# Up projection with the weights stationary and 256 token columns moving

## Chip, cores and metric

One core of a Trainium2 chip runs the whole kernel in one launch. The metric is the device time in microseconds; lower is better.

## Reference, cut to what matters

x is (1, 256, 2048), all in float32: 256 tokens, 2048 channels. After the token mixers, which the change does not touch, the channel mixer is

```python
h = rmsnorm(x, g_ffn_pre[l])
u = causal_dwconv(h @ w_up[l], ffn_conv_w[l])      # w_up: 2048 x 11264, 3 taps over the tokens
gate, val = jnp.split(u, 2, axis=-1)               # 5632 channels each
x = x + rmsnorm((jax.nn.silu(gate) * val) @ w_down[l], g_ffn_post[l])
```

rmsnorm divides each token's row by its root mean square. The kernel multiplies the un-normalised rows, and applies the token's factor r_h2 to the product.

## The kernel before

Every projection is made from three products of float32r parts: w is split into w_hi (rounded to float32r) and w_lo (the rest), and so are the activations; the product is hi*hi + hi*lo + lo*hi. Weights stream from memory in blocks of 256 x 512 (512 KB) through rings of four buffers: SyncE loads `raw`, ScalarE writes `w_hi` (line 415), VectorE writes `w_lo` (line 670), TensorE multiplies. A buffer of `raw` is free again when `w_lo` is written, one of `w_hi` and `w_lo` when the multiplication of four blocks earlier is done (`block_done`).

`multiply` (line 987) takes one block: for each of its 2 groups of 128 input channels and each of the 2 tiles of 128 tokens, three matmuls with a 128x128 tile of the transposed activations as stationary operand and 512 weight columns as moving operand: 12 matmuls a block, each with its own weight load. The result is 128 tokens x 512 channels in a PSUM bank, tokens on partitions.

The up projection runs in 11 steps (`up_step`), each with a half of 512 gate channels and a half of 512 value channels, 8 blocks a half, so 176 blocks. The convolution runs over tokens and wants channels on partitions. So each half takes this way: ScalarE copies the two banks to `up_stage`, scaled by r_h2 (`up_evacuate`, line 584, 2 instructions); TensorE turns it with 8 transposes of 128x128 into `TURN` in PSUM (`up_turn`, line 1159, placed behind the second block of the next half); ScalarE makes the first tap from it (`up_first_tap`, line 591, 4 instructions); VectorE adds the other two taps (`turned_conv`, line 703, 8 instructions). After both halves come silu (line 636), the product (906) and its split into act_hi (606) and act_lo (909), which the down projection reads. Gate and value halves have their own PSUM banks (`ACC[0]`, `ACC[1]`).

The order of work on each engine is written by hand: these steps stand at fixed places i = 0..7 between the block splits of the following half. The last `up_turn` stands inside the first chunk of the down projection. Before step 0, x is renewed, turned (line 1185) and split into h2_hi, h2_lo (the buffers of hT_hi, hT_lo, whose names the trace shows), and GpSimd works out r_h2 (line 366).

Of the kernel before, what the change touches and what calls it, by code (L numbers as in the profile page):

```python
# [7 lines left out]
ALU = mybir.AluOpType  # L8
# [3 lines left out]
P = 128  # L12
NT = 2
# [3 lines left out]
KB = 2  # L17
# [6 lines left out]
def build_block_kernel(nc, x, mem, g_mix_pre, w_in, w_gate, b_gate, conv_w, w_conv_out,  # L24
# [47 lines left out]
    with ExitStack() as ctx:  # L72
        def sem(name):
            return ctx.enter_context(nc.semaphore(name))
# [11 lines left out]
        def at(name, offset, shape, dt=F32):  # L86
            return nc.alloc_sbuf_tensor_at(name, shape, dt, offset=base + offset)
# [105 lines left out]

        act_hi = at("act_hi", RB, [P, FK, TOK], F32R)
        act_lo = at("act_lo", RB + 44 * K, [P, FK, TOK], F32R)
        up_stage = at("up_stage", RB + 88 * K, [P, NT, CW])
# [37 lines left out]
        d_inv, d_scaled, d_a, d_aT, d_aT_sb, d_o = (sem(n) for n in ("d_inv", "d_scaled", "d_a", "d_aT", "d_aT_sb", "d_o"))  # L234
        d_sq, d_ms, d_r, d_on, d_oT, d_hi, d_lo = (sem(n) for n in ("d_sq", "d_ms", "d_r", "d_on", "d_oT", "d_hi", "d_lo"))
        gate_ready, gated_sum, mix_hi = (sem(n) for n in ("gate_ready", "gated_sum", "mix_hi"))
        mix_sq, mix_sum, x_new, h2_sq = (sem(n) for n in ("mix_sq", "mix_sum", "x_new", "h2_sq"))
        silu_done, prod_done, act_hi_done, act_lo_done = (sem(n) for n in ("silu_done", "prod_done", "act_hi_done", "act_lo_done"))
        down_sq, down_y, down_sum, out_ready, out_stored = (sem(n) for n in ("down_sq", "down_y", "down_sum", "out_ready", "out_stored"))
# [163 lines left out]
        def _(act):  # L403
# [177 lines left out]
                    if i == 5 and c == 0:  # L581
                        merge_hi(NCH - 1)

            def up_evacuate(k, n_end, parity):
                act.wait_ge(turned_done, k)
                act.wait_ge(block_done, n_end)
                for t in range(NT):
                    last = nc.scalar.activation(up_stage[:, t, :], ACC[parity][:, t, :], ACT.Copy, scale=r_h2[:, t:t + 1])
                last.then_inc(evacuated[parity], 1)

            def up_first_tap(k, dst, blk):
                act.wait_ge(turned_done, k + 1)
                for b in range(BPC):
                    last = nc.scalar.activation(dst[:, b, :], TURN[:, b, :], ACT.Copy, scale=up_taps[:, 2, bass.ds(blk + b, 1)])
                last.then_inc(tap0, 1)

            def value_done(j, i):

                if i == 3:
                    up_evacuate(T_UP + 2 * j + 1, N_UP + 2 * CB * j + 2 * CB, 1)  # L600
                if i == 5:
                    act.wait_ge(prod_done, AHEAD + j)
                    up_first_tap(T_UP + 2 * j + 1, conv_v, FK + BPC * j)
                if i == 7:
                    act.wait_ge(prod_done, AHEAD + j + 1)
                    nc.scalar.activation(act_hi[:, bass.ds(BPC * j, BPC), :], prod[:], ACT.Copy).then_inc(act_hi_done, 1)

            def up_step(j, jp):
                n = N_UP + 2 * CB * j
                for i in range(CB):  # L610
                    split(n, i)
                    if jp is not None:
                        value_done(jp, i)
                    elif i == 2:

                        mix_squares(NCH - 1)
                        for g in range(NCH):
                            prepare(2 * NCH + g, g, (SCORE_T, TURN)[g % 2], g_ffn_v, h2_hi)
                        for t in range(NT):
                            act.wait_ge(mix_sq, NT * NCH + t)  # L620
                            last = nc.scalar.activation(junk_wide[:], x_res[:, t, :], ACT.Square, accum_out=sq_h2[:, t:t + 1])
                            last.then_inc(mix_sq, 1)
                        act.wait_ge(mix_sq, NT * NCH + NT)
                for i in range(CB):
                    split(n, CB + i)
                    if i == 3:
                        if jp is None:
                            act.wait_ge(rms_ready, 4)
                        up_evacuate(T_UP + 2 * j, n + CB, 0)
                    if i == 5:  # L630
                        if jp is not None:
                            act.wait_ge(prod_done, AHEAD + j)
                        up_first_tap(T_UP + 2 * j, conv_g, BPC * j)
                    if i == 6:
                        act.wait_ge(turned_read, T_UP + 2 * j + 1)
# [30 lines left out]
        def _(dve):  # L666
            def split(n, i, inc=1):

                dve.wait_ge(hi_ready, n + i + 1)
                nc.vector.tensor_tensor(w_lo[i % RING][:], raw[i % RING][:], w_hi[i % RING][:].bitcast(F32),  # L670
                                        ALU.subtract).then_inc(lo_ready, inc)
# [43 lines left out]

            def conv_count(k):

                if isinstance(k, int) and k < T_UP:
                    return [TI[("cv", 0)], TI[("cv", 1)]].index(k)
                return k - T_UP + 2  # L720

            def after_projection(c, i):
                name, half = proj[c]
# [164 lines left out]
            for c in range(NCH):  # L888
                for i in range(CB):
# [6 lines left out]
                    if i == 5 and c == 0:  # L896
                        merge_lo(NCH - 1)

            def value_done(j, i):
                if i == 5:  # L900
                    turned_conv(T_UP + 2 * j + 1, conv_v, lambda m, b: up_taps[:, m, bass.ds(FK + BPC * j + b, 1)])
                if i == 6:
                    dve.wait_ge(turned_read, T_UP + 2 * j + 2)
# [30 lines left out]
            def up_step(j, jp):  # L934
                n = N_UP + 2 * CB * j
                for i in range(CB):
                    split(n, i)
                    if jp is not None:
                        value_done(jp, i)
                    elif i == 2:  # L940
                        new_x()
                for i in range(CB):
                    split(n, CB + i)
                    if i == 5:
                        turned_conv(T_UP + 2 * j, conv_g, lambda m, b: up_taps[:, m, bass.ds(BPC * j + b, 1)])

            up_step(0, None)
            with dve.Fori(1, NUP) as j:
# [37 lines left out]
        def _(pe):  # L986
# [169 lines left out]
                    if i == 1 and c == 0:  # L1156
                        turn_merged(T_MERGE + NCH - 1)

            def up_turn(k, parity, count):
                pe.wait_ge(evacuated[parity], count)  # L1160
                pe.wait_ge(turned_read, k)
                turn(up_stage, TURN, turned_done)

            def up_step(j, jp):
                n = N_UP + 2 * CB * j
                pe.wait_ge(evacuated[0], E_UP + j)
                for i in range(CB):
                    if jp is None:
                        pe.wait_ge(prep_lo, 4 * NCH + i + 1)
                    multiply(n, i, CB, h2_hi, h2_lo, lambda t: ACC[0][:, t, :])  # L1170
                    if i == 1 and jp is not None:
                        up_turn(T_UP + 2 * jp + 1, 1, E_UP + jp + 1)
                pe.wait_ge(evacuated[1], E_UP + j)
                for i in range(CB):
                    multiply(n + CB, i, CB, h2_hi, h2_lo, lambda t: ACC[1][:, t, :])
                    if i == 1:
                        up_turn(T_UP + 2 * j, 0, E_UP + j + 1)

            for g in range(NCH):
                if g % 2:  # L1180
# [18 lines left out]
            pe.wait_ge(evacuated[0], E_DN)  # L1199
            down_chunk(0, lambda t: PS[:, t, :])  # L1200
            pe.wait_ge(turned_read, T_UP + 2 * NUP)
# [26 lines left out]
```

## Time and profile before

| | us |
|---|---|
| median of 3 runs (1712.16 to 1712.39) | 1712.18 |
| profiled execution, span from first to last instruction | 1710.7 |
| TensorE matmuls, busy | 1681.2 (98%) |
| TensorE weight loads, busy | 1389.9 (81%) |
| VectorE, busy | 956.0 (56%) |
| ScalarE, busy | 808.0 (47%) |
| DMA engines, share of the span | 59.2% |

The span is 1.5 us shorter than the median of the runs: that much lies around it. A matmul's duration in the trace is longer than the distance to the start of the next, because matmuls are pipelined; what a stream of them costs is read from the starts. TensorE's work therefore has to be counted by starts, not by busy time. Weight loads have a row of their own, PEld, beside the matmuls. A float32 matmul (not float32r) is recorded as two passes; a transpose as one.

### The profile page before, as it was taken

The numbers are of one execution on the slowest core, as the hardware profiler recorded it, in microseconds if no ns is written. First come the engines' busy times: TensorE is split into PE (matmuls) and PEld (weight loads), VectorE is DVE, ScalarE is ACT, GpSimd is POOL, SyncE is SP. The second block draws the span as 40 slices with busy tenths as digits, with TensorE's granted clock in tenths as the row PEclk, the third lists the DMA queues.
The fourth block names the chain that finished last, engine by engine and source line by source line (L and its number), as shares of the span: only waits on it lengthen the run. The fifth ranks groups of instructions, "written<-read, shape, count | busy, mean of one in ns | idle before, by whom it ended". The sixth has DMA issues, their size and how long they took to land.

```text
span 1710.7 us, 21909 instructions
## 1 busy us (share of the span) xinstructions
PE 1681.2 (98%) x7645; PEld 1389.9 (81%) x7645; DVE 956.0 (56%) x1100; ACT 808.0 (47%) x1028; POOL 21.4 (1%) x49
## 2 busy tenths in 40 slices
PE   8999999999999999999999899999999999999997
PEld 6888888888888888888888688888888888888886
DVE  5554555544556656655555566665666666544544
ACT  5544444444444444444444455555555555443442
POOL 0000000000000000000000000000000000000000
PEclk9999999999999999999999899999999999999999
DMA  7656555666655655666555366666666665654653
GB/s 270 205 176 186 168 159 163 186 192 185 190 187 189 239 179 178 196 219 198 186 199 189 123 180 187 182 189 189 186 185 185 184 183 185 214 194 171 211 196 123
DMA packets 165518, 320.87 MB, mean 188 GB/s; under 512 B 10504, under 2 KB 10841, under 8 KB 164953
## 3 DMA queue, kind: packets, MB, share of 16 engines
q1 hardware_dynamic: 165433, 320.15, 59.2%
q8 instruction: 34, 0.56, 0.1%
q14 instruction: 19, 0.16, 0.0%
q10 hardware_dynamic: 32, 0.01, 0.0%
HBM read 318.02 MB, written 2.10 MB: 187 GB/s over the span
## 4 chain that ended last, share of the span: by engine, by line
PE 95%; DVE 3%; ACT 1%; issue 1%; DMA 0%; DVEq 0%; ACTq 0%
PE PS L997 28%; PE PS L999 28%; PE PS L998 28%; PE PS L1140 3%; PE PS L1139 3%; PE PS L1138 3%; PE PS L1006 3%; ACT w_hi L415 0%; PE PS L1080 0%; PE PS L1065 0%; DVE y_down L979 0%; DMA mem_sb<-in_mem_dram 0%; ACT p_diff L540 0%; DVE x_res L925 0%; DVE gated L798 0%
## 5 line engine op out<-in xcount | busy, mean ns | idle before, releaser
L670 DVE TENSOR_TENSOR w_lo<-raw,w_hi 128x1024 fp32r<-128x1024 f32 x584 | 712.8, 1225 | 681.1 <-ACT w_hi L415 680.0
L415 ACT ACTIVATE w_hi<-raw 128x1024 fp32r<-128x1024 f32 x584 | 616.4, 1059 | 770.0 <-PE PS L999 717.2
L997 PE MATMUL PS<-w_hi,hT_hi 128*128 128x512 f32 x1536 | 606.1, 395 | 0.0
L999 PE MATMUL PS<-w_hi,hT_lo 128*128 128x512 f32 x1536 | 599.0, 390 | 0.0
L998 PE MATMUL PS<-w_lo,hT_hi 128*128 128x512 f32 x1536 | 598.3, 389 | 0.0
L999 PEld LDWEIGHTS PS<-w_hi,hT_lo 128*128 128x128 f32 x1536 | 288.6, 188 | 61.0
L997 PEld LDWEIGHTS PS<-w_hi,hT_hi 128*128 128x128 f32 x1536 | 288.9, 188 | 60.5 <-issue 2.7
L998 PEld LDWEIGHTS PS<-w_lo,hT_hi 128*128 128x128 f32 x1536 | 289.0, 188 | 58.1
L997 PE MATMUL PS<-w_hi,act_hi 128*128 128x512 f32 x352 | 137.2, 390 | 0.0
L999 PE MATMUL PS<-w_hi,act_lo 128*128 128x512 f32 x352 | 137.0, 389 | 0.0
L998 PE MATMUL PS<-w_lo,act_hi 128*128 128x512 f32 x352 | 136.9, 389 | 0.0
L997 PEld LDWEIGHTS PS<-w_hi,act_hi 128*128 128x128 f32 x352 | 66.1, 188 | 14.2 <-issue 0.6
L999 PEld LDWEIGHTS PS<-w_hi,act_lo 128*128 128x128 f32 x352 | 66.1, 188 | 13.7
L998 PEld LDWEIGHTS PS<-w_lo,act_hi 128*128 128x128 f32 x352 | 66.1, 188 | 13.6
L997 PE MATMUL PS<-w_hi,memT_hi 128*128 128x512 f32 x128 | 51.6, 403 | 1.5 <-DVE w_lo L670 0.9
L999 PE MATMUL PS<-w_hi,memT_lo 128*128 128x512 f32 x128 | 50.8, 397 | 0.0
L998 PE MATMUL PS<-w_lo,memT_hi 128*128 128x512 f32 x128 | 50.8, 397 | 0.0
L997 PE MATMUL PS<-w_hi,mixT_hi 128*128 128x512 f32 x128 | 49.9, 390 | 0.0
L999 PE MATMUL PS<-w_hi,mixT_lo 128*128 128x512 f32 x128 | 49.8, 389 | 0.0
L998 PE MATMUL PS<-w_lo,mixT_hi 128*128 128x512 f32 x128 | 49.8, 389 | 0.0
L997 PEld LDWEIGHTS PS<-w_hi,memT_hi 128*128 128x128 f32 x128 | 24.6, 192 | 7.0 <-issue 1.3
L999 PEld LDWEIGHTS PS<-w_hi,memT_lo 128*128 128x128 f32 x128 | 24.6, 192 | 5.3
(172 smaller groups left out, 1111.5 us busy)
## 6 DMA issues: line engine op xcount, KB each, us to landing
raw<-in_w_up_dram SPq DMA_DIRECT2D x176, 512.0 KB, 4.4
raw<-in_w_in_dram SPq DMA_DIRECT2D x112, 512.0 KB, 3.7
raw<-in_w_gate_dram SPq DMA_DIRECT2D x96, 512.0 KB, 4.1
raw<-in_w_down_dram SPq DMA_DIRECT2D x88, 512.0 KB, 4.2
raw<-in_w_mem_kv_dram SPq DMA_DIRECT2D x32, 512.0 KB, 4.1
raw<-in_w_o_dram SPq DMA_DIRECT2D x32, 512.0 KB, 3.6
raw<-in_w_conv_out_dram SPq DMA_DIRECT2D x16, 512.0 KB, 3.5
raw<-in_w_cross_out_dram SPq DMA_DIRECT2D x16, 512.0 KB, 3.7
```

The lines of the kernel that those rows point to most:

```text
L415: nc.scalar.activation(w_hi[i % RING][:], raw[i % RING][:], ACT.Copy).then_inc(hi_ready, inc)
L670: nc.vector.tensor_tensor(w_lo[i % RING][:], raw[i % RING][:], w_hi[i % RING][:].bitcast(F32), ALU.subtract).then_inc(lo_ready, inc)
L997: nc.tensor.matmul(o, a_hi, b_hi, start=first, stop=False)
L998: nc.tensor.matmul(o, a_hi, b_lo, start=False, stop=False)
L999: last = nc.tensor.matmul(o, a_lo, b_hi, start=False, stop=last_k)
L1006: last = nc.tensor.transpose(dst[:, b, t * P:(t + 1) * P], src[:, t, b * P:(b + 1) * P], ident[:])
L1138: nc.tensor.matmul(ACC[1][:, t, :], hi[:, k, s], w_hi[i % RING][:, c, :], start=k == 0, stop=False)
L1139: nc.tensor.matmul(ACC[1][:, t, :], hi[:, k, s], w_lo[i % RING][:, c, :], start=False, stop=False)
L1140: last = nc.tensor.matmul(ACC[1][:, t, :], lo[:, k, s], w_hi[i % RING][:, c, :], start=False, stop=k == HK - 1)
```

## The change

In the up projection alone, operands change places: a 128x128 tile of w_hi or w_lo is the stationary operand, and the 256 tokens of h2 move. The output has 128 channels on partitions and 256 tokens in half a PSUM bank. `multiply_up` issues for each block 2 groups of input channels x 4 groups of output channels x 3 products = 24 matmuls of 256 columns, each with its weight load, where `multiply` issued 12 of 512. Transposes, `up_stage` and its two ScalarE copies a half go. r_h2 now varies along the free axis, so it has to be a row that is the same on all partitions: once, VectorE writes two diagonal matrices, TensorE multiplies them with ones (float32, 2 matmuls of 128 columns), and ScalarE copies the row out of PSUM (`r_row`). VectorE then scales each half with one instruction over 128x1024 (`up_scale`, at i == 2), PSUM to SBUF. The taps read this SBUF copy and not PSUM; the first tap moves from i == 5 to i == 4. The down projection is as before, but for the transposes that stood in its first chunk.

```diff
+        up_scaled_sb = at("up_scaled_sb", RB + 88 * K, [P, BPC, TOK])
...
+        UP = [PS[:, 2 * h:2 * h + 2, :].rearrange("p b (c t) -> p (b c) t", t=TOK) for h in range(2)]
...
-            def up_evacuate(k, n_end, parity):
-                act.wait_ge(turned_done, k)
-                act.wait_ge(block_done, n_end)
-                for t in range(NT):
-                    last = nc.scalar.activation(up_stage[:, t, :], ACC[parity][:, t, :], ACT.Copy, scale=r_h2[:, t:t + 1])
-                last.then_inc(evacuated[parity], 1)
...
             def up_first_tap(k, dst, blk):
-                act.wait_ge(turned_done, k + 1)
+                act.wait_ge(up_scaled, k + 1)
                 for b in range(BPC):
-                    last = nc.scalar.activation(dst[:, b, :], TURN[:, b, :], ACT.Copy, scale=up_taps[:, 2, bass.ds(blk + b, 1)])
+                    last = nc.scalar.activation(dst[:, b, :], up_scaled_sb[:, b, :], ACT.Copy, scale=up_taps[:, 2, bass.ds(blk + b, 1)])
                 last.then_inc(tap0, 1)
...
+                    if i == 0 and jp is None:
+                        act.wait_ge(r_row_turned, 1)
+                        nc.scalar.activation(r_row[:], PS[:, 4, 0:TOK], ACT.Copy).then_inc(r_row_done, 1)
...
+            def up_scale(k, n_end, half):
+
+                dve.wait_ge(block_done, n_end)
+                if isinstance(k, int) and k == 0:
+                    dve.wait_ge(r_row_done, 1)
+                nc.vector.tensor_tensor(up_scaled_sb[:], UP[half], r_row[:, None, :].to_broadcast([P, BPC, TOK]),
+                                        ALU.mult).then_inc(up_scaled, 1)
+
+            def up_conv_taps(k, dst, taps):
+
+                dve.wait_ge(tap0, k + 3)
+                for b in range(BPC):
+                    last = nc.vector.scalar_tensor_tensor(out=dst[:, b, 1:TOK], in0=up_scaled_sb[:, b, 0:TOK - 1], scalar=taps(1, b),
+                                                          in1=dst[:, b, 1:TOK], op0=ALU.mult, op1=ALU.add)
...
+                    elif i == 4:
+
+                        dve.wait_ge(rms_ready, 4)
+                        nc.vector.memset(ones[:], 1.0)
+                        for t in range(NT):
+                            last = nc.vector.tensor_scalar(r_diag[:, t, :], ident[:], r_h2[:, t:t + 1], None, ALU.mult)
+                        last.then_inc(r_diag_done, 1)
...
-            def up_turn(k, parity, count):
-                pe.wait_ge(evacuated[parity], count)
-                pe.wait_ge(turned_read, k)
-                turn(up_stage, TURN, turned_done)
+            def multiply_up(n, i, half):
+
+                pe.wait_ge(lo_ready, n + i + 1)
+                for c in range(KB):
+                    k = KB * i + c
+                    for b in range(BPC):
+                        s = slice(b * P, (b + 1) * P)
+                        o, last_k = UP[half][:, b, :], k == DK - 1
+                        b_hi, b_lo = w_hi[i % RING][:, c, s], w_lo[i % RING][:, c, s]
+                        nc.tensor.matmul(o, b_hi, h2_hi[:, k, :], start=k == 0 and b % 2 == 0, stop=False, skip_group_check=True)
+                        nc.tensor.matmul(o, b_hi, h2_lo[:, k, :], start=False, stop=False, skip_group_check=True)
+                        last = nc.tensor.matmul(o, b_lo, h2_hi[:, k, :], start=False, stop=last_k, skip_group_check=True)
+                last.then_inc(block_done, 1)
...
+                    multiply_up(n, i, 0)
+                    if jp is None and i == CB - 1:
+
+                        pe.wait_ge(r_diag_done, 1)
+                        for t in range(NT):
+                            last = nc.tensor.matmul(PS[:, 4, t * P:(t + 1) * P], ones[:], r_diag[:, t, :], start=True, stop=True)
+                        last.then_inc(r_row_turned, 1)
...
-                    if i == 1 and isinstance(j, int):
-                        up_turn(T_UP + 2 * NUP - 1, 1, E_UP + NUP)
```

## Rows read from the trace of the kernel before

**Rows 1.** Page, part 1: busy us (share of the span) x instructions.

```profile
PE 1681.2 (98%) x7645; PEld 1389.9 (81%) x7645; DVE 956.0 (56%) x1100; ACT 808.0 (47%) x1028; POOL 21.4 (1%) x49
```

**Rows 2.** Page, part 2: TensorE clock granted, tenths, 40 slices.

```profile
PEclk9999999999999999999999899999999999999999
```

**Rows 3.** Page, part 4: chain that ended last, shares by engine.

```profile
PE 95%; DVE 3%; ACT 1%; issue 1%; DMA 0%; DVEq 0%; ACTq 0%
```

**Rows 4.** Groups by line and shape: count | busy us, mean ns | idle before.

```profile
L997 PE MATMUL PS<-w_hi,hT_hi 128*128 128x512 f32 x1536 | 606.1, 395 | 0.0
...
L1006 PE MATMUL PS<-ident,up_stage 128*128 128x128 f32 x176 | 22.8, 272 | 0.0
```

**Rows 5.** Timeline, TensorE, in an up step: start us, us, instruction.

```profile
1000.20 0.39 PE L997 MATMUL PS<-w_hi,hT_hi 128*128 128x512 f32 x1
...
1003.83 0.39 PE L998 MATMUL PS<-w_lo,hT_hi 128*128 128x512 f32 x1
```

**Rows 6.** Timeline, weight loads beside those matmuls.

```profile
1000.21 0.19 PEld L998 LDWEIGHTS PS<-w_lo,hT_hi 128*128 128x128 f32 x1
1000.43 0.19 PEld L999 LDWEIGHTS PS<-w_hi,hT_lo 128*128 128x128 f32 x1
```

**Rows 7.** Stretches: us, busy by engine, PEclk, DMA share, GB/s; an up stretch.

```profile
1000.00:1100.00 100.00, 100.00 (x459) 83.12 (x458) 60.12 (x72) 53.47 (x66) 0.00 (x0) 1.00 0.63 188
```

**Rows 8.** Timeline, TensorE, around one group of transposes.

```profile
1010.86 0.39 PE L999 MATMUL PS<-w_hi,hT_lo 128*128 128x512 f32 x1
1011.09 1.03 PE L1006 MATMUL PS<-ident,up_stage 128*128 128x128 f32 x8
1011.88 0.48 PE L997 MATMUL PS<-w_hi,hT_hi 128*128 128x512 f32 x1
1012.19 0.40 PE L998 MATMUL PS<-w_lo,hT_hi 128*128 128x512 f32 x1
```

**Rows 9.** Timeline, TensorE, first matmuls of up step 0.

```profile
960.32 0.63 PE L998 MATMUL PS<-w_lo,hT_hi 128*128 128x512 f32 x1
...
962.03 0.63 PE L999 MATMUL PS<-w_hi,hT_lo 128*128 128x512 f32 x1
```

**Rows 10.** Stretch of those matmuls: the eighth figure is the clock.

```profile
960.30:962.40 2.10, 2.10 (x6) 1.65 (x5) 1.40 (x4) 2.10 (x5) 0.00 (x0) 0.50 0.00 0
```

**Rows 11.** Timeline, weight loads with 128-column float32 matmuls, then float32r ones.

```profile
455.99 0.30 PEld L1123 LDWEIGHTS PS<-v_tok,a_diffT 128*128 128x128 f32 x2
456.21 0.30 PEld L1124 LDWEIGHTS PS<-v_tok,a_diffT 128*128 128x128 f32 x2
456.43 0.19 PEld L997 LDWEIGHTS PS<-w_hi,hT_hi 128*128 128x128 f32 x1
456.55 0.19 PEld L998 LDWEIGHTS PS<-w_lo,hT_hi 128*128 128x128 f32 x1
```

**Rows 12.** Timeline, TensorE, the same place: float32 passes of 128 columns.

```profile
455.88 0.38 PE L1122 MATMUL PS<-v_tok,a_diffT 128*128 128x128 f32 x2
...
456.32 0.39 PE L1124 MATMUL PS<-v_tok,a_diffT 128*128 128x128 f32 x2
```

**Rows 13.** Groups by line and shape, 985 to 1460 us: VectorE and ScalarE.

```profile
L670 DVE TENSOR_TENSOR w_lo<-raw,w_hi 128x1024 fp32r<-128x1024 f32 x168 | 205.7, 1224 | 166.7 <-ACT w_hi L415 166.7
L415 ACT ACTIVATE w_hi<-raw 128x1024 fp32r<-128x1024 f32 x168 | 177.9, 1059 | 193.3 <-PE PS L999 193.3
...
L588 ACT ACTIVATE up_stage<-PS,r_h 128x512 f32<-128x512 f32 x41 | 25.7, 674 | 0.0
...
L707 DVE SCALAR_TENSOR_TENSOR conv_g<-PS,up_taps,conv_g 128x255 f32<-128x255 f32 x44 | 18.2, 476 | 4.2 <-ACT conv_g L594 4.2
...
L594 ACT ACTIVATE conv_g<-PS,up_taps 128x256 f32<-128x256 f32 x44 | 17.2, 475 | 0.0
```

**Rows 14.** One line of VectorE: a PSUM by SBUF product, 128x1024; min/median/max ns.

```profile
L746 DVE TENSOR_TENSOR y_tmp<-PS,convT x2: 1217/1217/1217, 291.0 to 313.6; 128x1024 f32<-128x1024 f32 x2
```

**Rows 15.** Timeline, GpSimd, then VectorE, start of up step 0.

```profile
966.27 0.69 POOL L366 TENSOR_TENSOR r_h<-mean_sq,minus_half 128x2 f32<-128x2 f32 x1
...
966.75 3.50 DVE L670 TENSOR_TENSOR w_lo<-raw,w_hi 128x1024 fp32r<-128x1024 f32 x3 [0.92 <-ACT w_hi L415]
```

More of the change, by code:

```diff
@@ L195, in build_block_kernel @@
         act_lo = at("act_lo", RB + 44 * K, [P, FK, TOK], F32R)
-        up_stage = at("up_stage", RB + 88 * K, [P, NT, CW])
+        up_scaled_sb = at("up_scaled_sb", RB + 88 * K, [P, BPC, TOK])
+        r_diag = at("r_diag", RB + 96 * K, [P, NT, P])
+        ones = at("ones", RB + 97 * K, [P, P])
+        r_row = at("r_row", RB + 104 * K + 2 * K, [P, TOK])
         conv_g = at("conv_g", RB + 92 * K, [P, BPC, TOK])
@@ L236, in build_block_kernel @@
         gate_ready, gated_sum, mix_hi = (sem(n) for n in ("gate_ready", "gated_sum", "mix_hi"))
+        r_diag_done, r_row_turned, r_row_done = (sem(n) for n in ("r_diag_done", "r_row_turned", "r_row_done"))
+        up_scaled, up_conv = sem("up_scaled"), sem("up_conv")
         mix_sq, mix_sum, x_new, h2_sq = (sem(n) for n in ("mix_sq", "mix_sum", "x_new", "h2_sq"))
@@ L716, in conv_count @@
             def conv_count(k):
-                if isinstance(k, int) and k < T_UP:
-                    return [TI[("cv", 0)], TI[("cv", 1)]].index(k)
-                return k - T_UP + 2
+                return [TI[("cv", 0)], TI[("cv", 1)]].index(k)
             def after_projection(c, i):
@@ L897, in _ @@
                         merge_lo(NCH - 1)
+            def up_scale(k, n_end, half):
[9 more added lines that the diff above has]
+                                                          in1=dst[:, b, 1:TOK], op0=ALU.mult, op1=ALU.add)
+                last.then_inc(tap1, 1)
+                dve.wait_ge(tap1, k + 3)
+                for b in range(BPC):
+                    last = nc.vector.scalar_tensor_tensor(out=dst[:, b, 2:TOK], in0=up_scaled_sb[:, b, 0:TOK - 2], scalar=taps(0, b),
+                                                          in1=dst[:, b, 2:TOK], op0=ALU.mult, op1=ALU.add)
+                last.then_inc(up_conv, 1)
             def value_done(j, i):
+                if i == 2:
+                    up_scale(2 * j + 1, N_UP + 2 * CB * j + 2 * CB, 1)
                 if i == 5:
-                    turned_conv(T_UP + 2 * j + 1, conv_v, lambda m, b: up_taps[:, m, bass.ds(FK + BPC * j + b, 1)])
+                    up_conv_taps(2 * j + 1, conv_v, lambda m, b: up_taps[:, m, bass.ds(FK + BPC * j + b, 1)])
                 if i == 6:
-                    dve.wait_ge(turned_read, T_UP + 2 * j + 2)
+                    dve.wait_ge(up_conv, 2 * j + 2)
                     dve.wait_ge(silu_done, j + 1)
@@ L941, in up_step @@
                         new_x()
+                    elif i == 4:
[4 more added lines that the diff above has]
+                        last.then_inc(r_diag_done, 1)
                 for i in range(CB):
                     split(n, CB + i)
+                    if i == 2:
+                        up_scale(2 * j, n + CB, 0)
                     if i == 5:
-                        turned_conv(T_UP + 2 * j, conv_g, lambda m, b: up_taps[:, m, bass.ds(BPC * j + b, 1)])
+                        up_conv_taps(2 * j, conv_g, lambda m, b: up_taps[:, m, bass.ds(BPC * j + b, 1)])
             up_step(0, None)
@@ L1157, in _ @@
                         turn_merged(T_MERGE + NCH - 1)
-            def up_turn(k, parity, count):
-                pe.wait_ge(evacuated[parity], count)
-                pe.wait_ge(turned_read, k)
-                turn(up_stage, TURN, turned_done)
+            def multiply_up(n, i, half):
+                pe.wait_ge(lo_ready, n + i + 1)
+                for c in range(KB):
+                    k = KB * i + c
+                    for b in range(BPC):
+                        s = slice(b * P, (b + 1) * P)
[5 more added lines that the diff above has]
+                last.then_inc(block_done, 1)
             def up_step(j, jp):
                 n = N_UP + 2 * CB * j
-                pe.wait_ge(evacuated[0], E_UP + j)
+                if jp is None:
+                    pe.wait_ge(evacuated[0], E_UP)
+                else:
+                    pe.wait_ge(up_scaled, 2 * jp + 1)
                 for i in range(CB):
@@ L1169, in up_step @@
                         pe.wait_ge(prep_lo, 4 * NCH + i + 1)
[L1170 to L1173, printed above, removed]
+                    multiply_up(n, i, 0)
[4 more added lines that the diff above has]
+                        last.then_inc(r_row_turned, 1)
+                if jp is None:
+                    pe.wait_ge(evacuated[1], E_UP)
+                else:
+                    pe.wait_ge(up_scaled, 2 * jp + 2)
                 for i in range(CB):
-                    multiply(n + CB, i, CB, h2_hi, h2_lo, lambda t: ACC[1][:, t, :])
-                    if i == 1:
-                        up_turn(T_UP + 2 * j, 0, E_UP + j + 1)
+                    multiply_up(n + CB, i, 1)
             for g in range(NCH):
```

20 lines of the change are left out of this document (7 added, 13 removed).

## Prediction

> **What bounds the kernel now.** I read the views in this order. Part 1 of the page shows TensorE busy 98% of the span and no other engine above 56% [rows 1]; the chain that ended last lies on TensorE for 95% [rows 3]; its clock is full nearly everywhere [rows 2]. So the kernel is a queue of matmuls, and an edit counts by what it does to that queue. In the groups by line the 512-column float32r matmuls have no idle time before them, and the transposes of the up stage have none either [rows 4]: those are paid in full. Then the timeline, for the price of one matmul. From 1000.20 to 1003.83 there are 16 steps from start to start, so one 512-column matmul costs 0.2267 us, not the 0.39 us of its record [rows 5]. Each has a weight load, which starts with the matmul before it and is recorded with 0.19 us [rows 6], so it is over before it is wanted. In an up stretch the clock is 1.00, DMA at 63% and VectorE at 60% [rows 7]: nothing else is close.
>
> **Removed: the transposes.** From the last matmul ahead of a group (1010.86) to the second one behind it (1012.19) are 1.33 us [rows 8]; two ordinary steps would be 0.45, so a group costs 0.88 us (8 transposes at about 0.11). There are 22 groups (176 transposes [rows 4]): 22 x 0.88 = 19.4 us less on the path. The ScalarE copies, 2 x 0.674 us a half [rows 13], are off the path and bring nothing.
>
> **Changed: the matmuls, which decide the case.** The up stage has 11 x 2 x 8 = 176 blocks. Before: 12 x 176 = 2112 matmuls x 0.2267 = 478.8 us. After: 24 x 176 = 4224 matmuls of 256 columns at a price P that the trace does not show, since all float32r matmuls in it have 512 columns. The columns streamed are the same, so the question is how the 0.2267 us splits into a part per column and a part per matmul.
> At half clock (0.50, the 1.2 GHz level [rows 10]) the steps are (962.03 - 960.32) / 4 = 0.4275 us [rows 9], which is 512 columns at one column a cycle with nothing above it. At 2.4 GHz one column a cycle would be 0.2134 us. The full-clock step has 0.0133 us above that. This excess is either
> a) per matmul (a start, or a clash with the one weight load that goes with each): P = 0.1067 + 0.0133 = 0.120 us, 4224 x 0.120 = 506.9 us, 28.1 us more;
> b) per column (a stream that can't quite be fed at full clock): P = 0.2267 / 2 = 0.1133 us, 478.8 us, no change.
> The bound below: a load must fit under a matmul. Loads with 128-column float32 passes follow each other at 0.11 us (455.99, 456.21, 456.43, two in each of the first two records), and the first float32r load is followed by the next after 0.12 [rows 11]; the passes themselves come every 0.11 us [rows 12]. So 0.111 us is the lowest P that I can defend: 4224 x 0.111 = 468.9 us, 9.9 less. The bound above: if stationary and moving reads share one path, 640 columns in 0.2267 us make 384 columns 0.136 us: 574.5 us, 95.7 more. The loads of rows 11 speak against this one, since they ran at their rate beside a stream.
> I take a). A hint for it: the step beneath which a transpose's load ran is 0.23 us (1010.86 to 1011.09 [rows 8]), and the steps behind a break are 0.23 too, so the excess moves with what surrounds a matmul, which a pure rate per column would not do. It is a weak hint, and b) keeps a good chance.
> The Trainium skill ("TensorE: Matmul & The Clock Gate", section "Wait — 56ns, not 53.3ns?") has a fixed cost of about 2.5 ns for each warm matmul, on top of columns / 2.4 GHz. As an estimate from that page P would be 0.109 us, the sum 461.4 us, and the kernel some 36 us faster with the transposes gone. The 512-column step of this trace, 0.2267 us, does not follow that figure (0.2158), so I don't forecast by it, and its result shares the chance of rival 2; what it says of the kind of the cost (per matmul) is my case a).
>
> **Added: the row of r_h2, once.** On TensorE 2 float32 matmuls of 128 columns, two passes each, 4 x 0.11 = 0.44 us [rows 12], with about 0.1 for the break: 0.5 us. The operands are early: r_h2 is ready at 966.96 and VectorE writes its third to fifth w_lo of this step from 966.75 [rows 15], so its three small instructions behind i == 4 come blocks ahead of the end of the half. ScalarE then waits at i == 0 of the second half, with the splits of that half's blocks 1 to 7 queued behind it, until the row is in PSUM. From the end of block 7: 0.65 us to the signal, a 128x256 copy 0.48, w_hi 1.06, w_lo 1.22 [rows 13], together 3.4 us. TensorE has the row's 0.5 us and block 0 of the second half, 24 x 0.120 = 2.9 us, that is 3.4 us before it needs this w_lo. I put 0.3 us for this race: 0.8 us in all. If it is lost outright, 1 us.
>
> **Added off the path: up_scale.** 22 VectorE products of 128x1024 from PSUM, 1.22 us each [rows 14], at i == 2. In the up stretch VectorE waits 166.7 us for ScalarE, and ScalarE 193.3 us for TensorE [rows 13], so both run ahead as far as the ring lets them; ScalarE loses 1.35 us a half. Queued behind the wait for the end of the last half is the w_lo of block 3. ScalarE may write w_hi of block 3 only when that same half has ended, so the wait ends before w_hi is there; w_lo then comes some 2.6 us after the end of the half, and TensorE wants it after three blocks, 8.2 us or more. The taps, 8 x 0.476 us as recorded [rows 13], stand where they stood. From SBUF they may be dearer or cheaper, by the rows as they are; a cover of 5 us a half is there for it. The scale has the PSUM bank free a whole half before TensorE writes it again. All of this costs nothing; were the cover gone, each half would be late by up to 1.2 us, 27 us over 22 halves.
>
> **The sum.** 1710.7 - 19.4 + 28.1 + 0.8 = 1720.2 us span; with the 1.5 us that lie around it, 1721.7 us against the median of 1712.18: slower by 0.6%. The point of no change is P = (478.8 + 19.4 - 0.8) / 4224 = 0.1177 us. What a measurement of this kernel can tell from no change is about 0.2%, 3.4 us, so "same" is P between 0.1169 and 0.1186, which none of the mechanisms gives.
>
> **Rivals.**
> 1. The excess is per column, P = 0.1133: 1710.7 - 19.4 + 0.0 + 0.8 + 1.5 = 1693.6 us, faster by 1.1%. This is the case on the other side. Its place is every matmul of the up stage, its gain the transposes, and it decides as soon as P is under 0.1169. For it: the half-clock steps show no excess at all [rows 9], as they would with a feed that just misses full rate, and steady steps all have the same length [rows 5]. Against: rows 8, as said.
> 2. The excess disappears with short matmuls and the load is the limit, P = 0.111: 1683.7 us. For it: float32 passes of 128 columns at 0.11 [rows 12]. Against: there the column rate is half (two passes, each slow enough to be fed), so they don't show the float32r stream at its full rate.
> 3. Load and stream disturb each other more when they overlap all the time and not half of it; P = 0.125, the excess grown by a third: 4224 x 0.125 = 528.0, and 1742.8 us. At the far end P = 0.136 gives 1789.3 us. For it: at 512 columns a load of some 0.11 us covers half the matmul, now all of it. Against: rows 11.
> 4. The engines beside TensorE come late (up_scale, taps): up to 27 us on top of case a), 1749 us. The waiting times of rows 13 speak against it.
> That the change doesn't do what it says I exclude: the transposes and the copies are gone from the code.
>
> **How the numbers follow.** Case a) 0.52, rival 1 0.26, rival 2 0.06, rival 3 0.12 (half of it with P under 0.123), rival 4 0.02, and 0.02 for a P that falls at no change. Faster 0.32, same 0.02, slower 0.66. The range from 1688 to 1735 us holds case a) with P up to 0.123 and rival 1 with its errors, and leaves out rivals 2 and 4 and the upper half of 3. The likeliest case has a range of its own, 1717 to 1728.
>
> **What would show it.** The start-to-start step of the new matmuls: 0.120 for a), 0.113 for rival 1, 0.111 for rival 2, above 0.122 for rival 3. Block ends 2.88 us apart against 2.72. No transposes of up_stage and no other wait of TensorE in the up stage than, at most once, the one behind the row. VectorE about 27 us busier, ScalarE about 30 less. The rest of the kernel step by step as before. I am wrong if the step isn't 0.120; the rest of the sum moves the time by 2 us at most.

## Result, and the profile after

The changed kernel takes 1719.57 us (median of 4 runs, 1718.85 to 1719.95) against 1712.17 us for the kernel before (median of 4): a ratio of 1.0047, 95% interval [1.0034, 1.0059]. It is 0.5% slower. The forecast was 1721.7 us. The profiled execution has a span of 1718.2 us, and took 1719.95 us, so 1.75 us lie around it.

The page after, in the parts that answer rows 1 to 3 (busy time by engine, granted clock, shares of the chain that ended last):

```profile
PE 1689.3 (98%) x9585; PEld 1482.5 (86%) x9585; DVE 980.2 (57%) x1125; ACT 784.7 (46%) x985; POOL 21.4 (1%) x49
...
PEclk9999999999999999999999899999999999999999
...
PE 95%; DVE 3%; ACT 1%; issue 1%; DMA 0%; DVEq 0%; ACTq 0%
```

TensorE is the bound as before, at the same clock. VectorE has 24.2 us more and ScalarE 23.3 us less (forecast: about 27 and 30), and neither shows in the time. The first tap, which now reads SBUF, takes ScalarE 496 ns where it took 475. The new matmuls are 4224 (3 x 1408), with no idle time ahead of them. That column starts at the end of the record before, and a record (0.28 us) is longer than a step, so a wait under 0.16 us doesn't show in it; the starts have to say that there is none. The groups by line, which answer rows 4 (the transposes of `up_stage` have no group any more):

```profile
L1194 PE MATMUL PS<-hT_hi,w_hi 128*128 128x256 f32 x1408 | 399.2, 283 | 0.0
...
L1194 PEld LDWEIGHTS PS<-hT_hi,w_hi 128*128 128x128 f32 x1408 | 270.8, 192 | 0.0
```

The price of one is read from the starts, as in rows 5. TensorE's timeline in an up step:

```profile
1049.78 0.28 PE L1194 MATMUL PS<-hT_hi,w_hi 128*128 128x256 f32 x1
...
1052.90 0.28 PE L1196 MATMUL PS<-hT_hi,w_lo 128*128 128x256 f32 x1
```

and the stretch, which answers rows 7:

```profile
1000.00:1100.00 100.00, 100.00 (x836) 100.00 (x835) 64.75 (x76) 47.20 (x55) 0.00 (x0) 1.00 0.63 185
```

The clock is 1.00 there, and no other engine is near its end. From 1049.78 to 1052.90 are 26 steps: 0.120 us each, case a) of the prediction to the last digit. From 962 us to the end of the stage only two steps of a 256-column matmul are longer than 0.13 us, both of 0.20 us at the row of r_h2 (see below).

Where the stage begins and ends, on TensorE's timeline after:

```profile
959.04 0.56 PE L1194 MATMUL PS<-hT_hi,w_hi 128*128 128x256 f32 x1
...
959.83 0.41 PE L1194 MATMUL PS<-hT_hi,w_hi 128*128 128x256 f32 x1
...
960.90 0.35 PE L1196 MATMUL PS<-hT_hi,w_lo 128*128 128x256 f32 x1
...
1467.38 0.40 PE L1023 MATMUL PS<-w_hi,act_hi 128*128 128x512 f32 x1
```

and before:

```profile
959.75 0.78 PE L997 MATMUL PS<-w_hi,hT_hi 128*128 128x512 f32 x1
...
1459.04 0.39 PE L997 MATMUL PS<-w_hi,act_hi 128*128 128x512 f32 x1
```

The up stage grew from 499.3 to 508.3 us. The down projection lost the one group of transposes that stood in it and became 0.8 us shorter, and the up stage began 0.7 us earlier. The change leaves the work ahead of it as it was, and the kernels of the experiments began the stage anywhere from 956.8 to 959.7 us, so I count that as chance. 9.0 - 0.8 - 0.7 gives the 7.5 us by which the spans differ.

The first matmuls run at a granted clock of 0.50. From 959.83 to 960.90 are 5 steps, 0.214 us each: 256 columns at one column a cycle, and two of them are one 512-column step of 0.4275 us. At half clock the cut into shorter matmuls costs nothing.

### The profile page after: what moved, and what is told of

Same layout as the page of the kernel before. It is cut to its first block, busy times and chain, and to the rows that moved or that the text cites. A ratio compares the mean times of both kernels' runs of the same rounds, so it can differ in the third digit from the quotient of the medians.

```text
span 1718.2 us, 25718 instructions
## 1 busy us (share of the span) xinstructions
PE 1689.3 (98%) x9585; PEld 1482.5 (86%) x9585; DVE 980.2 (57%) x1125; ACT 784.7 (46%) x985; POOL 21.4 (1%) x49
## 4 chain that ended last, share of the span: by engine, by line
PE 95%; DVE 3%; ACT 1%; issue 1%; DMA 0%; DVEq 0%; ACTq 0%
PE PS L1023 18%; PE PS L1025 18%; PE PS L1024 18%; PE PS L1194 10%; PE PS L1195 10%; PE PS L1196 10%; PE PS L1166 3%; PE PS L1165 3%; PE PS L1164 3%; PE PS L1032 1%; ACT w_hi L421 0%; PE PS L1106 0%; PE PS L1091 0%; DVE y_down L1005 0%; DMA mem_sb<-in_mem_dram 0%
## 5 line engine op out<-in xcount | busy, mean ns | idle before, releaser
L1194 PE MATMUL PS<-hT_hi,w_hi 128*128 128x256 f32 x1408 | 399.2, 283 | 0.0
L1195 PE MATMUL PS<-hT_lo,w_hi 128*128 128x256 f32 x1408 | 398.8, 283 | 0.0
L1196 PE MATMUL PS<-hT_hi,w_lo 128*128 128x256 f32 x1408 | 398.8, 283 | 0.0
L1023 PE MATMUL PS<-w_hi,hT_hi 128*128 128x512 f32 x832 | 329.5, 396 | 0.0
L1025 PE MATMUL PS<-w_hi,hT_lo 128*128 128x512 f32 x832 | 324.3, 390 | 0.0
L1024 PE MATMUL PS<-w_lo,hT_hi 128*128 128x512 f32 x832 | 323.9, 389 | 0.0
L1194 PEld LDWEIGHTS PS<-hT_hi,w_hi 128*128 128x128 f32 x1408 | 270.8, 192 | 0.0
L1195 PEld LDWEIGHTS PS<-hT_lo,w_hi 128*128 128x128 f32 x1408 | 270.7, 192 | 0.0
L1196 PEld LDWEIGHTS PS<-hT_hi,w_lo 128*128 128x128 f32 x1408 | 270.7, 192 | 0.0
L1024 PEld LDWEIGHTS PS<-w_lo,hT_hi 128*128 128x128 f32 x832 | 156.4, 188 | 31.2
L1023 PE MATMUL PS<-w_hi,memT_hi 128*128 128x512 f32 x128 | 51.4, 402 | 1.4 <-DVE w_lo L666 0.7
```

The costliest lines, as they stand in the source:

```text
L1023: nc.tensor.matmul(o, a_hi, b_hi, start=first, stop=False)
L1024: nc.tensor.matmul(o, a_hi, b_lo, start=False, stop=False)
L1025: last = nc.tensor.matmul(o, a_lo, b_hi, start=False, stop=last_k)
L1194: nc.tensor.matmul(o, b_hi, h2_hi[:, k, :], start=k == 0 and b % 2 == 0, stop=False, skip_group_check=True)
L1195: nc.tensor.matmul(o, b_hi, h2_lo[:, k, :], start=False, stop=False, skip_group_check=True)
L1196: last = nc.tensor.matmul(o, b_lo, h2_hi[:, k, :], start=False, stop=last_k, skip_group_check=True)
```

## Experiments

**The number of columns alone.** Is it the size of the matmul, or that the weights stand still? The kernel before, with its operands in their places, and each matmul of the up stage cut in two:

```diff
-                    multiply(n, i, CB, h2_hi, h2_lo, lambda t: ACC[0][:, t, :])
+                    multiply_split(n, i, h2_hi, h2_lo, 0)
...
+                        for q in range(2):
+                            m = slice(q * TOK, (q + 1) * TOK)
+                            o, b_hi, b_lo = ACC[half][:, t, m], w_hi[i % RING][:, c, m], w_lo[i % RING][:, c, m]
```

> The kernel before, with each up block as 24 matmuls of 256 weight columns (activations stationary, as before) in place of 12 of 512; transposes and all else kept. Theory (about 13 ns for every float32r matmul, whichever operand moves): 4224 matmuls at 0.120 us, 28 us more than before, about 1740 us. Rival (the 0.120 us of the changed kernel comes from its operand order, weight tiles as stationary operand and half-bank outputs of four channel groups): steps of 0.113 us, about 1712 us.

1738.19 us (4 runs) against 1711.12 (11 runs): ratio 1.0157 [1.0140, 1.0174], 27.1 us more. Its timeline on TensorE:

```profile
1099.86 0.28 PE L1013 MATMUL PS<-w_hi,hT_hi 128*128 128x256 f32 x1
...
1103.10 0.28 PE L1013 MATMUL PS<-w_hi,hT_hi 128*128 128x256 f32 x1
```

27 steps in 3.24 us: 0.120 again. The loss belongs to 256 columns a matmul; at this length, which operand moves is of no account.

**The transposes alone.** The kernel before with one transpose of eight a group:

```diff
-                turn(up_stage, TURN, turned_done)
+                nc.tensor.transpose(TURN[:, 0, 0:P], up_stage[:, 0, 0:P], ident[:]).then_inc(turned_done, 1)
```

> The kernel before with 1 of the 8 transposes of each up group (the other 7 channel-by-token tiles are left out, so the taps read stale values); the waits stay. Theory (the transposes stand in TensorE's queue and are paid in full): 22 x 7 x 0.109 = 16.8 us less, about 1695.4 us. Rival (they fill time in which TensorE would wait for something else): less than half of that, and a new wait behind the group.

1694.27 us, ratio 0.9902 [0.9885, 0.9918]: 16.8 us less, as expected, and no new wait of TensorE. So the loss by shorter matmuls is measured, 27 us, and so are 7/8 of the transposes, 16.8 us. The eighth and the breaks around a group were not removed alone. By the starts of the trace before, a group costs 0.91 us on average if the 20 matmuls behind it are taken in (21 groups, 0.89 to 0.93), for 22 groups 20.0 us. 27.1 - 20.0 and 0.5 for the row of r_h2 give 7.6 us, where the medians differ by 7.4.

**What the 13 ns are.** The step at 512 and at 256 columns has the same 13.3 ns above one column a cycle. To see whether that is a law or a coincidence, each block of a half got its own number of moving columns (cut):

```diff
+                        w = (256, 512, 384, 320, 256, 224, 192, 128)[i]
+                        o = PS[:, 2 * half + b // 2, :][:, 0:w]
```

> The changed kernel with another number of moving columns in each of the 8 blocks of a half (256, 512, 384, 320, 256, 224, 192, 128), so that its sums are not those of the up projection. Start-to-start steps read by block. Theory A (columns / 2.4 GHz + 13.3 ns per matmul, load floor 0.111): 0.2267, 0.173, 0.147, 0.120, then 0.111 for 224, 192 and 128. Theory B (0.4427 ns a column, and the 0.120 us at 256 columns is the pace of the weight loads): 0.2267, 0.170, 0.142, and 0.120 for 256 and all below. Time about 1805 us by either.

1806.94 us. This kernel and the next two ran once each, so their times have no interval; the argument rests on the steps in their traces, at a granted clock of 1.00 in all three from 1000 to 1100 us. First matmul of each block on TensorE's timeline, 24 matmuls apart:

```profile
1018.02 0.40 PE L1198 MATMUL PS<-hT_hi,w_hi 128*128 128x512 f32 x1
...
1023.49 0.33 PE L1198 MATMUL PS<-hT_hi,w_hi 128*128 128x384 f32 x1
...
1027.67 0.31 PE L1198 MATMUL PS<-hT_hi,w_hi 128*128 128x320 f32 x1
...
1031.19 0.28 PE L1198 MATMUL PS<-hT_hi,w_hi 128*128 128x256 f32 x1
...
1034.06 0.27 PE L1198 MATMUL PS<-hT_hi,w_hi 128*128 128x224 f32 x1
...
1036.74 0.26 PE L1198 MATMUL PS<-hT_hi,w_hi 128*128 128x192 f32 x1
...
1039.40 0.24 PE L1198 MATMUL PS<-hT_hi,w_hi 128*128 128x128 f32 x1
...
1042.05 0.33 PE L1198 MATMUL PS<-hT_hi,w_hi 128*128 128x256 f32 x1
```

Divided by 24: 0.228 us for 512 columns, 0.174 for 384, 0.147 for 320, 0.120 for 256, then 0.112, 0.111 and 0.110 for 224, 192 and 128. Columns / 2.4 GHz + 13.3 ns gives 0.2267, 0.1733, 0.1467 and 0.120: theory A holds from 512 to 256 columns, and below lies a floor of 0.111. Theory B, which would have 0.142 at 320 and 0.120 below 256, falls.

**Is it the weight load?** The same kernel with narrower stationary tiles in blocks 0 to 3 and again in 4 to 7:

```diff
+                        m = (128, 96, 64, 32, 128, 96, 64, 32)[i]
+                        o, b_hi, b_lo = o[0:m], b_hi[:, 0:m], b_lo[:, 0:m]
```

> The changed kernel with the stationary tile cut to 128, 96, 64 and 32 weight columns in blocks 0 to 3 and again in 4 to 7 (the other output channels are left out); 256 moving columns throughout. Theory A (a start cost of the matmul, not of its load): 0.120 us at all sizes, 1719.6 us. Theory B (the loads set the 0.120 us): steps of 0.113 us, the share by columns, for 96 columns and fewer; 3/4 of the matmuls 6.7 ns shorter, 21 us less. Theory C (a clash between the load's reads and the stream, so the excess goes with the size of the load): 0.117, 0.113, 0.110, some 19 us less.

1700.71 us, with 256 moving columns throughout. The form after the names is the stationary tile:

```profile
1004.12 0.28 PE L1196 MATMUL PS<-hT_hi,w_hi 128*128 128x256 f32 x1
...
1007.00 0.28 PE L1196 MATMUL PS<-hT_hi,w_hi 128*96 128x256 f32 x1
...
1009.78 0.28 PE L1196 MATMUL PS<-hT_hi,w_hi 128*64 128x256 f32 x1
...
1012.50 0.28 PE L1196 MATMUL PS<-hT_hi,w_hi 128*32 128x256 f32 x1
...
1015.22 0.28 PE L1196 MATMUL PS<-hT_hi,w_hi 128*128 128x256 f32 x1
```

0.120, 0.116, 0.113 and 0.113 us. Neither A (0.120 at all sizes) nor C (0.117, 0.113, 0.110) is right as written: a part of about 6.7 ns goes with the load once it is wider than 64 columns, and a part of 6.7 ns stays. Seen alone this says that half of the excess is a clash with the load. So a third kernel crossed both sizes (cut):

```diff
+                        w, m = ((256, 128), (512, 96), (512, 64), (512, 32), (256, 32), (128, 64), (128, 32), (384, 64))[i]
```

> The changed kernel with (moving columns, stationary columns) set for each of the 8 blocks of a half: (256, 128), (512, 96), (512, 64), (512, 32), (256, 32), (128, 64), (128, 32), (384, 64); its sums are not those of the up projection. The steps seen so far fit columns / 2.4 GHz + 6.7 ns for each matmul + up to 6.7 ns more when the load beneath has more than 64 columns, and a floor near 0.111 us. Theory A (the extra is a clash with the load, once per load): 0.220 for (512, 64) and (512, 32), 0.229 or so for (512, 96), 0.167 for (384, 64), and the floor falls with the load: 0.060 for (128, 64) and (128, 32). Theory B (the floor belongs to the matmul and not to the load): 0.111 for (128, 64) and (128, 32) too. Theory C (the 6.7 ns gained at 256 columns were those of a load that barely fits under its matmul, and a 512-column matmul hides it anyway): 0.2267 for all 512-column blocks.

1857.74 us. First matmuls of the blocks:

```profile
1022.84 0.39 PE L1199 MATMUL PS<-hT_hi,w_hi 128*96 128x512 f32 x1
...
1028.36 0.39 PE L1199 MATMUL PS<-hT_hi,w_hi 128*64 128x512 f32 x1
...
1033.88 0.40 PE L1199 MATMUL PS<-hT_hi,w_hi 128*32 128x512 f32 x1
1039.45 0.28 PE L1199 MATMUL PS<-hT_hi,w_hi 128*32 128x256 f32 x1
1042.19 0.22 PE L1199 MATMUL PS<-hT_hi,w_hi 128*64 128x128 f32 x1
1043.63 0.22 PE L1199 MATMUL PS<-hT_hi,w_hi 128*32 128x128 f32 x1
1045.07 0.34 PE L1199 MATMUL PS<-hT_hi,w_hi 128*64 128x384 f32 x1
1049.23 0.28 PE L1199 MATMUL PS<-hT_hi,w_hi 128*128 128x256 f32 x1
```

Two answers. The floor is the load's: 128 moving columns take 0.060 us with 64 or 32 stationary columns, where they took 0.110 with 128. But the clash doesn't carry over to long matmuls: with 96, 64 and 32 stationary columns the 512-column step is 0.230, 0.230 and 0.232 us, above the 0.2267 with a full load, and (384, 64) has 0.173. Theories A (0.220 at 512) and C (0.2267) both fall for the long matmuls; A's falling floor holds, and B falls. So with a narrow load (64 or 32 columns) the excess is 6.7 ns at 128 and 256 moving columns, 13.3 ns at 384 and 17 to 19 ns at 512; with a full load it is 13.3 ns from 256 to 512. As a sum for a start and a sum for a load this can't be written, and what makes it stays open.

The Trainium skill ("TensorE: Matmul & The Clock Gate", section "LDWEIGHTS (loading the stationary operand)") gives the nanoseconds of a load as its columns / 1.2; an estimate from it is 107 ns for 128 columns and 53 ns for 64. The floor of 0.110 to 0.112 us here lies 3 to 5 ns above the first. At 64 stationary columns the step of 0.060 us would fit the second too, but it is the same at 32, so there the load isn't what sets it.

**VectorE's cover.** The changed kernel with `up_scale` made three times:

```diff
+                for m in range(2):
+                    nc.vector.tensor_tensor(up_scaled_sb[:], UP[half], r_row[:, None, :].to_broadcast([P, BPC, TOK]),
+                                            ALU.mult).then_inc(up_extra, 1)
+                    dve.wait_ge(up_extra, 2 * k + m + 1)
```

> The changed kernel with up_scale issued three times over, 2 x 1.22 us more on VectorE for each half. Theory (VectorE's work is covered by the ring): no change from the changed kernel, 1719.6 us. Rival (VectorE's cover is thin, and the changed kernel already pays a part of its 1.22 us there): up to 22 x 2.4 = 54 us more, with waits of TensorE for w_lo or up_scaled.

1719.72 us, ratio 1.0051 [1.0034, 1.0068], against the kernel before: the changed kernel's time. Its groups by line from 985 to 1467 us (VectorE) show 42 more products, and where they went:

```profile
L666 DVE TENSOR_TENSOR w_lo<-raw,w_hi 128x1024 fp32r<-128x1024 f32 x170 | 205.7, 1222 | 103.2 <-ACT w_hi L421 103.2
L899 DVE TENSOR_TENSOR up_scaled_sb<-PS,r_row 128x1024 f32<-128x1024 f32 x42 | 51.4, 1224 | 12.0 <-PE PS L1200 11.3
```

In the changed kernel the first line reads:

```profile
L666 DVE TENSOR_TENSOR w_lo<-raw,w_hi 128x1024 fp32r<-128x1024 f32 x170 | 207.8, 1224 | 153.7 <-ACT w_hi L421 153.7
```

51.4 us of added work took 50.5 us out of VectorE's wait for w_hi. `up_scale` costs nothing, and rival 4 of the prediction is out.

**A kernel that keeps the gain.** If each start costs 13 ns, fewer and longer matmuls should pay. w_hi is the stationary operand twice, for h2_hi and for h2_lo; one matmul of 512 columns does both into the two halves of a bank, and the halves are added afterwards (ScalarE copies one, VectorE adds, then scales). A half now fills four banks, not two, and the row of r_h2 is made two blocks earlier, behind block 5 (cut):

```diff
-                        nc.tensor.matmul(o, b_hi, h2_hi[:, k, :], start=k == 0 and b % 2 == 0, stop=False, skip_group_check=True)
-                        nc.tensor.matmul(o, b_hi, h2_lo[:, k, :], start=False, stop=False, skip_group_check=True)
-                        last = nc.tensor.matmul(o, b_lo, h2_hi[:, k, :], start=False, stop=last_k, skip_group_check=True)
+                        nc.tensor.matmul(o, b_hi, h2_both[:, :, k, :], start=k == 0, stop=False, skip_group_check=True)
+                        last = nc.tensor.matmul(o[:, 0:TOK], b_lo, h2_hi[:, k, :], start=False, stop=last_k, skip_group_check=True)
```

> The changed kernel, with hi*hi and hi*lo made by one matmul of 512 moving columns (256 of h2_hi, 256 of h2_lo) into the two halves of a bank, added afterwards by one ScalarE copy and one more VectorE instruction a half; 16 matmuls a block, not 24. Theory (13 ns for each matmul): a block takes 8 x (0.2267 + 0.120) = 2.77 us against 2.88, 176 blocks 18.7 us less than the changed kernel, about 1701 us, 0.65% under the kernel before. Rival (a moving operand in two pieces pays the start for each piece, or the cost is by columns): no gain, about 1720 us. Second rival: the added work of VectorE and ScalarE is not covered, waits of TensorE at the half boundaries, up to 22 x 2 us.

1704.58 us, ratio 0.9968 [0.9949, 0.9987] against the kernel before: 0.3% faster than that, and 0.8% than the changed kernel. But its 8 runs fall into two groups, four from 1699.8 to 1701.5 and four from 1707.6 to 1711.6. I first blamed late w_lo, and moved the second VectorE instruction of a half from i == 2 to i == 3; beside it the first version ran again:

> The kernel with one 512-column matmul for both hi parts, its second VectorE instruction moved behind the w_lo of block 3 (i == 3 in place of i == 2), so that this w_lo comes 1.22 us earlier. The earlier kernel showed times from 1699.8 to 1711.6 us. Theory (a thin cover of w_lo at the half boundary makes the late ones, through loads of raw that start late): all runs near 1700 us. Rival (the spread comes from elsewhere, as the place of the buffers or the loads themselves): the same spread.

> The same kernel as e4_both, beside e4b_late on one chip. If its spread belongs to the kernel, times from 1700 to 1711 us again; if it belonged to the chip of that call, about 1701 us in all runs.

The moved version has 1701.84 us (0.9952 [0.9935, 0.9968]), with two of 6 runs at 1707.6 and 1710.0; the first version 1706.08 us (0.9966 [0.9951, 0.9982]), with 6 of 12 runs from 1709.8 to 1711.1. The two groups are there in both, so the cover theory falls. The two profiled executions of the first version happened to be one of each kind, with no wait of TensorE in the up stage in either and a granted clock of 1.00 from 1000 to 1400 us in both. TensorE's timeline over 19 pairs of matmuls, in the one of 1699.7 us:

```profile
1100.20 0.39 PE L1205 MATMUL PS<-h_both,w_hi 128*128 128x512 f32 x1
...
1106.79 0.39 PE L1205 MATMUL PS<-h_both,w_hi 128*128 128x512 f32 x1
```

and in the one of 1709.2 us:

```profile
1100.16 0.40 PE L1205 MATMUL PS<-h_both,w_hi 128*128 128x512 f32 x1
...
1106.87 0.40 PE L1205 MATMUL PS<-h_both,w_hi 128*128 128x512 f32 x1
```

6.59 us against 6.71: a pair takes 0.347 us, just 0.2267 + 0.120, or 0.353. Over 11 x 2 x 8 x 8 = 1408 pairs the difference is 9 us, the distance of the groups. The stream itself has two rhythms. The profiled execution of the moved version (1707.62 us) has 0.353 too, and began its up stage 2.7 us earlier.

The rhythm can change inside one execution, so it isn't the chip, the place of the buffers or the order of the code alone that sets it. In the trace of 1709.2 us the pairs ahead of the row of r_h2, which is a break in the stream, are of the short kind:

```profile
965.33 0.39 PE L1205 MATMUL PS<-h_both,w_hi 128*128 128x512 f32 x1
...
976.77 0.39 PE L1205 MATMUL PS<-h_both,w_hi 128*128 128x512 f32 x1
...
977.46 0.61 PE L1224 MATMUL PS<-r_diag,ones 128*128 128x128 f32 x4
```

33 pairs in 11.44 us are 0.347 each; from behind the row to the down projection they take 0.353. The moved version does the same. The trace of 1699.7 us has 0.347 on both sides, and the profiled execution of the in-turn kernel with one piece (below) has 0.353 ahead of the row and 0.347 behind it. So in these four traces a stretch keeps its rhythm up to 480 us long, and where it changed it changed at this break; what decides there isn't shown. Three more kernels looked for what admits the slow one: the four 512-column matmuls first and then the four of 256; h2_hi and h2_lo side by side, so that the 512 columns lie in one piece; and both.

> The kernel with one 512-column matmul for both hi parts, with the four 512-column matmuls of an input-channel group issued first and the four of 256 columns behind them, not in turn. In the profiles of the version in turn the 512-column step is 0.230 us in one execution (span 1699.7 us) and 0.236 us in another (1709.2 us), with no wait in either. Theory (the alternation of lengths lets the stream fall into one of two rhythms; equal neighbours hold the steps of 0.2267 and 0.120 seen in the other kernels): 693 us per thousand pairs, all runs near 1701 us. Rival (two moving pieces per matmul are what admits the slower rhythm, whatever the order): the same two groups of times, near 1701 and 1710 us.

(Its figure for the sum should be 347 us per thousand pairs.)

> The kernel e4_both, with h2_hi and h2_lo of each channel block stored side by side, so that the 512 moving columns lie in one piece; order in turn (512, 256). Theory (the slower rhythm needs a moving operand in two pieces): steps 0.2267 and 0.120, all runs near 1701 us. Rival (the rhythm comes from neighbours of unequal length): the two groups, near 1701 and 1710 us, again.

> The same side-by-side storage with the order of e8_grouped (four of 512 columns, then four of 256). Theory of the two pieces: the 512-column steps fall from 0.234 to 0.2267, all runs near 1701 us. Rival (what slows the 512-column steps there is something else, as the banks they walk over): 0.234 again, about 1707 us.

Grouped: 1707.23 us, 0.9976 [0.9967, 0.9986], all ten runs from 1706.1 to 1708.3. One piece, in turn: 1702.46 us, 0.9963 [0.9947, 0.9979], five of 8 runs from 1700.7 to 1702.7 and three from 1709.1 to 1711.0. One piece, grouped: 1707.26 us, 0.9973 [0.9962, 0.9984], all seven from 1706.1 to 1707.6. The grouped timeline:

```profile
1099.88 1.09 PE L1203 MATMUL PS<-h_both,w_hi 128*128 128x512 f32 x4
1100.81 0.63 PE L1207 MATMUL PS<-h_both,w_lo 128*128 128x256 f32 x4
1101.28 1.09 PE L1203 MATMUL PS<-h_both,w_hi 128*128 128x512 f32 x4
```

Four pairs take 1.401 or 1.406 us, changing throughout the stage, 0.351 a pair on average from 1000 to 1400 us and between the two rhythms; the trace of the one-piece grouped kernel has the same average, and its 512-column steps stay at 0.234. The pieces are of no account, with either order. The order is: in turn gives two rhythms, grouped gives one time in between. The expected 0.2267 + 0.120 was missed by the grouped kernels. What sets the rhythm is not settled: the banks over which the matmuls walk were named as a rival and not tried, and neither was a kernel without the break.

## Why the prediction was right

- **The bound.** TensorE's queue, read from starts. It held: no wait of TensorE in the up stage after the change but one of 0.08 us (see the row of r_h2), and all else hidden.
- **The price P.** The step on which all hung. Forecast 0.120 us, measured 0.120. Rivals 1 (0.113), 2 (0.111) and 3 (0.125) are out for this shape, and so is the 0.109 that the prediction sets beside them. The bound of 0.111 below, taken from float32 passes, turned out to be a real floor, met at 224 columns and fewer. Since float32r matmuls of 128 columns have it too (0.110), the 0.11 us of the float32 passes doesn't show the halved column rate that rival 2 reads into it. At half clock there is no excess at 256 columns either (0.214 us); the prediction counts that absence in favour of rival 1, and rival 1 is wrong all the same. But the reason given for P, an excess of one kind per matmul, is only half true: it fits all full loads from 256 to 512 columns, and the crossed sizes show that it isn't one fixed cost. The number was right because 256 columns with a full load lie on the same line as 512.
- **The hint for a).** I read the steps of 0.23 us behind a break as the excess moving with its surroundings. The two rhythms of the last kernels show that such movement exists (a pair can be 0.347 us ahead of a break and 0.353 behind it, or the other way round); it speaks for neither a) nor rival 1. It was the only reason given for a) over rival 1, so the choice between 1721.7 and 1693.6 us was in good part luck.
- **The transposes.** Forecast 0.88 us a group, 19.4 in all; 7 of 8 transposes were worth 16.8 us, as forecast for that kernel. The price was a little low: the steps behind a group stay longer than 0.2267 us for a while, which two steps don't show, and over 20 a group costs 0.91 us.
- **The row of r_h2.** Forecast 0.5 us and 0.3 for the race with w_lo. TensorE's timeline after, at the end of the first half:

```profile
982.91 0.28 PE L1196 MATMUL PS<-hT_hi,w_lo 128*128 128x256 f32 x1
983.03 0.61 PE L1213 MATMUL PS<-r_diag,ones 128*128 128x128 f32 x4
983.40 0.36 PE L1194 MATMUL PS<-hT_hi,w_hi 128*128 128x256 f32 x1
983.60 0.28 PE L1195 MATMUL PS<-hT_lo,w_hi 128*128 128x256 f32 x1
```

  From 982.91 to 983.60 are 0.69 us where two steps are 0.24: 0.45 us. Then the race. ScalarE and VectorE behind it,

```profile
983.68 0.38 ACT L625 ACTIVATE r_row<-PS 128x256 f32<-128x256 f32 x1 [7.96 <-PE PS L1213]
...
985.04 2.36 DVE L666 TENSOR_TENSOR w_lo<-raw,w_hi 128x1024 fp32r<-128x1024 f32 x2 [8.07 <-ACT w_hi L421]
```

  end the first of these two w_lo at 986.27 us. TensorE's weight loads at the border of block 0 and block 1 of the second half:

```profile
986.12 0.19 PEld L1196 LDWEIGHTS PS<-hT_hi,w_lo 128*128 128x128 f32 x1
986.32 0.19 PEld L1194 LDWEIGHTS PS<-hT_hi,w_hi 128*128 128x128 f32 x1
```

  They are 0.20 us apart, not 0.12, and so are the two matmul starts there (986.35 and 986.55). The race was lost by 0.08 us, too little for the view of waits. The row costs 0.53 us in all, where 0.8 was forecast.
- **The sum.** The spans differ by 7.5 us, forecast 9.5. Of the 2.0 us, 0.7 lie ahead of the up stage, 0.3 in the row, and about 0.5 in the matmuls at half clock: 7 of 512 columns before, some 9 of 256 after, which the sum had as equal. The rest, about 0.5 us, fits what the groups of transposes cost above 0.88 us each (20.0 us, not 19.4). None of these terms decided the case.

## What to carry to other kernels

When a matmul is cut into shorter ones, the columns stay and the starts double: read the start-to-start step at the length that the trace has, take off one column a cycle, and charge the rest to each matmul. Here 2112 more matmuls at 13.3 ns each, 28 us, were worth more than 176 transposes, 20 us. This held at full clock, with full weight loads, from 512 down to 256 columns; below that the step stopped at the 0.111 us of the load. If two matmuls share a stationary tile, try to make them one with a longer moving operand: here that took the kernel from 0.5% slower to 0.3% faster. And measure such a kernel in many runs: a stream without a wait can have two rhythms, and a break in it can change the one for the other.

## What the runs showed of the hardware that was not expected

- Float32r, full clock, 128 stationary columns: 0.228, 0.174, 0.147 and 0.120 us for 512, 384, 320 and 256 moving columns, 0.110 to 0.112 for 224 and fewer. With 64 or 32 stationary columns: 0.113 for 256 and 0.060 for 128, but 0.230 and 0.232 for 512, longer than with a full load. At half clock 256 columns take 0.214 us, with nothing above one column a cycle.
- 512- and 256-column matmuls in turn run at 0.347 or at 0.353 us a pair, without a wait. A stretch between breaks keeps its rhythm, up to 480 us long; at the break by two float32 matmuls the pair grew in two of four traces, shrank in one and stayed in one. Four and four run at 0.351 on average.
